# Expert rows weighed by five products on TensorE and one multiply-add on VectorE, with the fourth tile's diagonals made late

## The reference, cut to what matters

```
scores = jax.nn.sigmoid((x2 @ w_router).astype(jnp.float32))
_, idx = lax.top_k(scores + router_bias.astype(jnp.float32), TOP_K)      # TOP_K = 6
gate = gate / jnp.sum(gate, axis=-1, keepdims=True) * ROUTED_SCALE
...
yb = hb @ w_down[eb]
return acc.at[tok_b].add((yb * gate_b[:, None]).astype(acc.dtype)), None
...
shared = (jax.nn.silu(x2 @ w_sh_gate) * (x2 @ w_sh_up)) @ w_sh_down
return acc[:T] + shared
...
x = layer_norm(DEEPNORM_ALPHA * x + ffn, ln2_g[i], ln2_b[i])
```

## Time and profile before

| | us |
|---|---|
| median of 3 runs (lowest, highest) | 2092.46 (2089.9, 2094.02) |
| the profiled execution: its own time | 2090.71 |
| its span | 2089.0 |
| mean granted clock of TensorE in the span | 0.967 |
| TensorE busy, matmuls | 1881.8 |
| VectorE busy | 800.2 |
| ScalarE busy | 367.5 |

### The profile page before, as it was taken

How to read it: one execution, slowest core, us unless ns; L and a number is a source line. 1 busy time by engine, 2 the same in 40 slices (tenths; PEclk the granted TensorE clock), 3 DMA queues, 4 the chain that set the end, 5 groups by cost and what they waited for, 6 DMA issues and landing times. The chain is left out here.

```text
span 2089.0 us, 33051 instructions
## 1 busy us (share of the span) xinstructions
PE 1881.8 (90%) x11184; PEld 1118.2 (54%) x11185; DVE 800.2 (38%) x2137; ACT 367.5 (18%) x830; POOL 294.6 (14%) x385
## 2 busy tenths in 40 slices
PE   9999899779999989788999689999888999987787
PEld 4475435456666546444444368865455666554443
DVE  2100654523333323226367754524623333322226
ACT  2000650101111101010344322110101111110010
POOL 6000000011111111110017331200011111111110
PEclk9999999989999999999999689999899999999999
DMA  7220215399999999995222110025689999999997
GB/s 242 79 63 0 92 69 219 146 410 398 421 420 421 420 421 420 421 357 215 81 61 77 31 33 2 1 81 208 259 329 373 396 422 422 422 423 423 423 382 289
DMA packets 144044, 541.61 MB, mean 259 GB/s; under 512 B 30902, under 2 KB 68370, under 8 KB 94174
## 3 DMA queue, kind: packets, MB, share of 16 engines
q1 hardware_dynamic: 122654, 490.20, 58.6%
q0 software_dynamic: 21312, 50.37, 6.3%
HBM read 521.58 MB, written 46.14 MB: 272 GB/s over the span
## 5 line engine op out<-in xcount | busy, mean ns | idle before, releaser
L663 PE MATMUL bank<-W,XT 128*64 128x256 f32 x2816 | 328.6, 391 | 53.0 <-DMA W<-in_w_exp_gate_dram 20.8
L663 PEld LDWEIGHTS bank<-W,XT 128*64 128x64 f32 x2816 | 229.2, 141 | 164.3 <-issue 39.3
L698 PE MATMUL bank<-W,ht 128*64 128x512 f32 x704 | 162.5, 603 | 14.9 <-DMA W<-in_w_exp_down_dram 11.0
L1985 PE MATMUL bank<-XT,room 128*128 128x512 f32 x352 | 157.5, 602 | 0.0
L674 DVE TENSOR_TENSOR sig<-sig,bank 128x256 f32<-128x256 f32 x72 | 30.3, 421 | 282.1 <-ACT sig L670 282.0
L663 PE MATMUL bank<-room,XT 128*64 128x256 f32 x896 | 105.3, 387 | 11.8 <-DMA room<-in_w_exp_gate_dram 6.7
L676 DVE TENSOR_TENSOR h<-sig,bank 128x256 f32<-128x256 f32 x72 | 30.4, 422 | 219.4 <-PE bank L663 219.3
L1985 PEld LDWEIGHTS bank<-XT,room 128*128 128x128 f32 x352 | 66.8, 193 | 84.4 <-issue 84.0
L663 PE MATMUL bank<-third_high,XT 128*64 128x256 f32 x896 | 102.5, 380 | 8.5 <-DMA third_high<-in_w_exp_up_dram 8.5
L698 PE MATMUL bank<-third_high,ht 128*64 128x512 f32 x448 | 102.3, 597 | 8.4 <-DMA third_high<-in_w_exp_down_dram 5.5
L649 ACT ACTIVATE XT<-bank 128x512 f32<-128x512 f32 x74 | 44.2, 597 | 336.5 <-PE bank L641 336.5
(11 more groups left out here) (438 smaller groups left out, 2728.6 us busy)
## 6 DMA issues: line engine op xcount, KB each, us to landing
W<-in_w_exp_gate_dram SPq DMA_DIRECT2D x88, 1024.0 KB, 25.6
W<-in_w_exp_up_dram SPq DMA_DIRECT2D x88, 1024.0 KB, 27.5
W<-in_w_exp_down_dram SPq DMA_DIRECT2D x88, 1024.0 KB, 27.4
room<-in_w_exp_gate_dram SPq DMA_DIRECT2D x40, 1024.0 KB, 23.8
third_high<-in_w_exp_up_dram SPq DMA_DIRECT2D x40, 1024.0 KB, 25.0
third_high<-in_w_exp_down_dram SPq DMA_DIRECT2D x40, 1024.0 KB, 25.1
W<-y_rows SPq DMA_DIRECT2D x8, 2048.0 KB, 21.4
room<-in_rwkv_w_in_dram SPq DMA_DIRECT2D x22, 512.0 KB, 4.1
```

The source lines that it names most:

```text
L663: last = pe.matmul((gate, up)[m][64 * a:64 * a + 64, :], xt[s][:, k, 64 * a:64 * a + 64], weights(w, a, m)[:, k * FE:(k + 1) * FE], start= ...
L698: last = pe.matmul(B[5 + half][64 * a:64 * a + 64, :], ht[:, j, 64 * a:64 * a + 64], weights(w, a, 2)[:, at:at + 512], start=(j == 0), sto ...
L1985: last = pe.matmul(main(i)[:], wc[i % WBUFS][:, kb, :], K.XT[:, kb, :], start=(kb == 0), stop=(kb == KD - 1))
```

## The change

BY_VECTOR goes from 2 to 1, and so BY_TENSOR from 4 to 5. With five rows per tile, four tiles would need 20 squares where there is room for 16, so the room now holds three tiles (15 squares), and the fourth tile's five diagonals are written over the first tile's, after TensorE has finished with these (`summed` at 2). TensorE now waits for the diagonals of each tile ahead of that tile's products. The lines below the new function stand 6 lines further down than before, so L1011, L1030 and L1040 are L1017, L1036 and L1046.

```diff
-BY_VECTOR = 2
+BY_VECTOR = 1
 BY_TENSOR = TOPK - BY_VECTOR
...
-        self.diagonal = room[:, 0, :].rearrange("p (t j q) -> p t j q", t=NT, j=BY_TENSOR)
+        self.diagonal = room[:, 0, 0:(NT - 1) * BY_TENSOR * P].rearrange("p (t j q) -> p t j q", t=NT - 1, j=BY_TENSOR)
...
-        pe.wait_ge(self.diagonals, NT * BY_TENSOR)
         for t in range(NT):
+            pe.wait_ge(self.diagonals, (t + 1) * BY_TENSOR)
             pe.wait_ge(self.loaded_t[t], 16)
             for half in range(2):
                 for j in range(BY_TENSOR):
-                    last = pe.matmul(B[2 * t + half][:], self.diagonal[:, t, j, :],
+                    last = pe.matmul(B[2 * t + half][:], self.diagonal[:, t % (NT - 1), j, :],
                                      self.rows[:, t, BY_VECTOR + j, half * 512:(half + 1) * 512],
                                      start=False, stop=(j == BY_TENSOR - 1))
...
     def scale(self, act):
         K = self.K
-        for t in range(NT):
+        def diagonals(t):
             for j in range(BY_TENSOR):
-                act.activation(self.diagonal[:, t, j, :], K.ident[:], ACT.Copy,
+                act.activation(self.diagonal[:, t % (NT - 1), j, :], K.ident[:], ACT.Copy,
                                scale=K.gates[:, t, BY_VECTOR + j:BY_VECTOR + j + 1]).then_inc(self.diagonals, 1)
+
+        for t in range(NT - 1):
+            diagonals(t)
         for t in range(NT):
             self.ln.root(act, t)
+            if t == 0:
+                act.wait_ge(self.summed, 2)
+                diagonals(NT - 1)
             if self.tiles is not None and t:
                 self.tiles.copy(act, t - 1)
```

## The result

The changed kernel takes 2097.36 us (median of 20 runs, 2093.58 to 2100.64), the kernel before 2089.48 (20 runs, 2083.8 to 2097.0). The ratio is 1.0033, with a 95% interval of 1.0024 to 1.0042: 6.9 us slower, between 5.0 and 8.8. The direction came out, and the time lies 0.14 us under the range.

The account below looks back on a forecast made before the run. VectorE was taken as bound by a little, with rows and TensorE close behind, and TensorE after the change. Layer 0 +6.03 and layer 1 +3.85 make 9.88 us on 2090.71, 2100.6, as a median 2102.3; range 2097.5 to 2106.0.

Parts of the forecast that it names:

- The direction: Whole kernel: slower with chance 0.92, the same 0.06, faster 0.02.
- TensorE becomes the bound in both layers: Both combinations: two more matmuls cost TensorE 1.72 us per tile, 8.59 us or 9.46 with transposes, slowest of three.
- The rival that TensorE has room: Combinations: fifth product runs in the matmuls' shadow, tile stays 6.87 us, no change at 2093.6 median; chance 0.06.
- The relief of VectorE shows nowhere: Combinations: VectorE's tile falls 1.30 us, from 8.16 to 6.86, but it then waits for TensorE ahead of every second add.
- Rows one row's time later: Row loads in both combinations: five rows ahead of TensorE's semaphore instead of four, so its rows land 1.28 us later.
- Diagonals at nothing: ScalarE's diagonals: the last five cost 1.5 us behind tile 0's root but are hidden; without cover 1.5 us per layer.
- The clock dip behind layer 0: Behind layer 0's last tile: TensorE idles 4.3 us and the clock again halves, as before the change.
- the rival that it goes: Behind layer 0's last tile: no clock dip, 3.4 us come back, time 2098.9; chance 0.17.
- I let all of it through.: Behind layer 0: its +6.03 us loss passes whole through last transposes, barrier and next stage to the end.
- The median of the runs shown, 2092.46: Base of the forecast: 1.75 us added to the profiled execution's sum, 2100.6, giving 2102.3, 0.47% slower.

Follow-up runs that it names:

- experiment 2: Changed kernel with two rows on VectorE again, loads as before, and a fifth TensorE product with a diagonal of zeros: 1.0033 of the kernel before, 6.9 us slower.
- 5: Changed kernel with rows loaded as before (four, then two) and TensorE's fifth product last in each half: combinations of 55.67 and 53.38 us.
- Experiment 6: Kernel before with VectorE's second multiply-add left out and nothing in its place: 0.9998 in time, combinations of 50.99 and 49.65 us.
- experiment 1: Changed kernel with two rows on VectorE again, keeping the new waits and late diagonals: 1.0001 of the kernel before.
- six delays: Kernel before with extra ScalarE activations, five variants behind layer 0's last copy, one ahead of layer 1's last root; the latter lengthened its combination 7.25 us, time 6.3.
- 24.47 us: Kernel before with 75 extra activations behind ScalarE's last copy of layer 0, a delay of 24.47 us: 23.8 us (20.7 to 27.0) more time.
- 3.68: Kernel before with 14 extra activations behind ScalarE's last copy of layer 0, a delay of 3.68 us: 1.5 us (-0.6 to 3.3) more time.
- 8.45: Kernel before with 28 extra activations behind ScalarE's last copy of layer 0, a delay of 8.45 us: 5.0 us (2.9 to 6.9) more time.
- Kernels 12: Kernel before with VectorE weighing 3, 2, 1, 2 rows, TensorE's rows awaited singly, VectorE's rows loaded first in every tile: 0.9992 in time.
- kernel 13: Kernel before with VectorE weighing 3, 2, 1, 2 rows, TensorE's awaited singly, VectorE's loaded first in tile 0 alone: 0.9969, 2084.76 us.
- 8: Kernel before with VectorE weighing 3, 2, 1, 2 rows and TensorE's rows awaited one by one, VectorE's rows loaded last: 0.9999 in time.

## Why the prediction was right and wrong, point by point

- **TensorE becomes the bound in both layers.** Right: 0.43 us per record, 9.46 us per tile in layer 0. The rival that TensorE has room, read from the weight loads' 37% of busy time, is out by experiment 2 (+7.5 us in the combinations): the even spacing of the records decided. VectorE waits for TensorE in every tile, from tile 1 on 1.64 us in layer 1 and up to 2.53 in layer 0, where I had said 1.5 and 2.4.
- **The relief of VectorE shows nowhere.** Right in the sum, and shown by experiments 2 and 5, which end alike with and without it. Experiment 6 shows why: even alone it was worth only 0.9 us.
- **Rows one row's time later.** Right at tile 0: counted from the first shared product, 1.08 us later in layer 0, and in layer 1 at +14.26 us, where the prediction had +14.30. Wrong at tile 1 of layer 1: I had its rows 23.46 us behind the first shared product and a wait of 0.57 us, but TensorE went on at 22.85 without one; why the rows were there sooner isn't shown. This term was 0.6 us too large, and with it layer 1 (+3.85 forecast, +3.18 measured). Layer 0 was +6.03 forecast, +5.79 measured.
- **Diagonals at nothing.** Right (experiment 1).
- **The clock dip behind layer 0.** It stayed, so the rival that it goes is out.
- **"I let all of it through."** Within the intervals for four of six delays, that of 24.47 us among them, and not for those of 3.68 and 8.45. For the change itself, 8.97 us of combinations stand against 6.9 (5.0 to 8.8) of time, 0.2 us outside. The stretch between was 1.8 us shorter in the changed kernel's trace, well inside its scatter of 6.4 us. I had given that scatter no room of its own.
- **"The median of the runs shown, 2092.46, is 1.75 above that execution, so for a median I say 2102.3."** This is the step that failed. Over 20 runs, of which the three shown are the first, the kernel before has a median of 2089.48, 3.0 us lower than over the three alone. On that base my sum gives 2099.4, and the range shifted with it would be 2094.5 to 2103.0, which holds 2097.36. On the four chips of the experiments the kernel before had medians of 2090.66 to 2091.87, under 2092.46 too. I carried the sample error of three runs into the forecast whole and allowed 2 us for it. The other 2 us: 0.9 are the two layers (0.2 and 0.7 too large), and 1.1 is what was in the combinations but not in the difference of the medians. The mechanism was right and the sizes of these terms were not; without the 3.0 us of the base, the other 2 would have stayed inside the range.

What stays open is why the delays of 3.68 and 8.45 us, and by a hair the change, cost less than they added: a fixed part that comes back, or scatter of stretches that no kernel touches. Kernels 12 and 13 speak for the scatter, but nothing settles it; it would take more traces of each kernel.

## What to carry to other kernels

Before work is moved off the engine that has no gaps, leave it out altogether and see what the stage gives back: here 0.9 us in two stages, because the next slower of TensorE and the rows took only 0.4 to 0.5 us per tile less than VectorE (7.74 and 7.7 against 8.16), while the work cost TensorE 1.72 us per tile. Here three resources run at nearly one pace, and the win lay in the first tile, where VectorE waited for rows that it could have had earlier: the rows shared 3, 2, 1 and 2, awaited one by one, with VectorE's three first in tile 0, took 3.9 us off the two combinations (2.7 of it by the order alone, kernel 13 against 8) and 0.31% off the time. And a median of three is no base for a forecast of half a per cent.

## What the runs showed of the hardware that I had not expected

A pause of TensorE of 1.20 us, at the same place of the same instructions, was followed by a granted clock of 0.50 for some 3 us in one trace and by 1.00 in another; the untouched millisecond around it varied by 6.4 us over 18 traces, nearly as much as the whole change. What decides whether such a drop comes is not shown.
